# Sparse attention's pairs: the order of TensorE's step, and one PSUM bank for both heads of a narrow pair

## The chip, the cores and the metric

The kernel runs on one core of one Trainium2 chip. The metric is the time of an execution on the device in microseconds, the median of three. TensorE (PE), with its weight loads (PEld), VectorE (DVE), ScalarE (ACT), GpSimd (POOL) and SyncE (SP), which only issues transfers, run side by side and meet at semaphores.

## The reference

The program is two transformer blocks with several mixers, on 512 tokens of width 1024. The change touches one mixer of the second block, a sparse attention of 16 heads in 4 groups. It has three branches: over compressed blocks, over selected blocks, and over a window. With 512 tokens there are 8 blocks to select from and up to 16 are taken, and the window is 512 wide, so the selected and the window branch both come to causal attention over all keys, each with keys, values and a gate of its own. Cut to these two:

```python
q = q.reshape(B, S, G, Hg, dk) * dk ** -0.5            # 4 groups of 4 heads, dk = 64
gates = jax.nn.sigmoid(gl).reshape(B, S, G, Hg, 3)
...
p_sel = masked_softmax(jnp.einsum('bghtd,bgtkd->bghtk', qg, k_g), (pos <= t[:, None])[:, :, None])
o_sel = jnp.einsum('bghtk,bgtkd->btghd', p_sel.astype(v_g.dtype), v_g)
...
# the window: the same with k_w and v_w; then
# o = gates[0] * o_cmp + gates[1] * o_sel + gates[2] * o_win
```

## The kernel before

Everything is computed in fp32 with operands split into a high part (rounded) and a low part (the remainder), so that a product is made of two or three products of TensorE. In the stage in question (about 1034 to 1179 us of the profiled run) the work is cut into 64 **pairs**: the list `npairs` runs over 4 groups g, 4 query tiles t of 128 rows, 2 pairs of heads hp and the 2 branches b. Pair p has two heads, units 2p and 2p + 1 (`v_` in the code). A query tile t sees t + 1 key blocks of 128, so pairs 0 to 3 of a group work on 128 columns, 4 to 7 on 256, 8 to 11 on 384 and 12 to 15 on 512. The first two kinds are called narrow below, the others wide.

What happens to a pair, and the name of the semaphore that tells of it:

- `scores(p)` (PE): for each head two products for the high and low part of the keys and one that adds the mask, into one of two sets of PSUM banks, 0 and 1 or 2 and 3 (`p_scored`);
- reduce (DVE): the negative maximum over both heads (`p_peaked`);
- exponentials (ACT): one instruction for each head, which also sums (`p_exped`);
- scaling (POOL): the reciprocal of the sums, then one multiplication for each head (`p_scaled`);
- `turn(p)` (PE): transposes the t + 1 blocks of each head, the first head into bank 4, the second into bank 5, whatever the pair (`p_turned`);
- high (ACT): copies the transposed head, rounded, to `nprobT` (`p_high`); low (DVE): bank minus `nprobT` to `nprobL` (`p_low`), head by head; both tiles hold two pairs;
- `values(p)` (PE): products of both with the values, into banks 6 and 7, summed over the two branches (`p_summed`);
- after every second pair two additions (DVE) onto `oT`, which already holds the compressed branch (`p_added`).

There is no planner here: each engine has a loop written by hand over steps s, and its instructions run in that order. TensorE's step is values(s-4), scores(s+1), turn(s-2). ScalarE's is high(s-3), then the exponentials of s. VectorE's is reduce(s), low(s-3), and in even steps the additions. GpSimd goes through the heads one by one. `turn(p)` waits for the scaling of its head and for low of the same head of pair p-1, whose bank it writes. high(p) and low(p) also wait until values(p-2) have been computed, whose slot of `nprobT` and `nprobL` they overwrite. The stage before is the compressed branch, the one after it the output projection, whose weights are on their way already.

Of the kernel before, what the change touches and what calls it, by code (L numbers as in the profile page):

```python
# [23 lines left out]
ALU = mybir.AluOpType  # L24
ACT = mybir.ActivationFunctionType
AXX = mybir.AxisListType.X

P = 128
# [139 lines left out]
def build(nc, w, out):  # L168

    ctx = ExitStack()  # L170
    with ctx:
# [19 lines left out]
        bank = [psum[:, i, :] for i in range(8)]  # L191
# [16 lines left out]
        ident = const[:, C_ID:C_ID + P]  # L208
# [173 lines left out]
        class NormTiles:  # L382
# [60 lines left out]
            def turn(self, pe, t):  # L443

                for c in range(2):
                    pe.wait_ge(self.scaled, 2 * t + c + 1)
                    if t >= 2:
                        pe.wait_ge(self.low, 2 * (t - 2) + c + 1)
                    for i in range(4):
                        d = 4 * c + i  # L450
                        mm = nc.tensor.transpose(self.banks[2 * (t % 2) + c][:, i * P:(i + 1) * P],  # L451
                                                 self.h[:, t % 2, d * P:(d + 1) * P], ident)
                    mm.then_inc(self.turned, 1)
# [404 lines left out]
        for t in range(NT):  # L858
            for hp in range(FOX_H // 2):
                wd = (t + 1) * P  # L860
# [1469 lines left out]
        nprobL = nsa_tile("nprobL", [P, 4, S], 71424, F32R)  # L2330
        nprob = nsa_tile("nprob", [P, 8, S], 79616)
        nprobT = nsa_tile("nprobT", [P, 4, S], 96000, F32R)
# [406 lines left out]
        npairs = [(g, t, hp, b) for g in range(NSA_G) for t in range(NT) for hp in range(2) for b in range(2)]  # L2739
        n_np = len(npairs)  # L2740
# [11 lines left out]

        minus_one = stat[:, 36:38]

        def sum_of(o):
            return bank[6 + o % 2][:, 0:2 * P]

# [3 lines left out]
        @block.tensor  # L2761
        def _(pe):
            def scores(p):
                g, t, hp, b = npairs[p]
                wd = (t + 1) * P
                if p % 16 == 0:
                    pe.wait_ge(k_twice[g], 64)
                if p >= 2:
                    pe.wait_ge(p_exped, 2 * p - 2)
                for i in range(2):  # L2770
                    _, _, h, kb = unit_of(2 * p + i)
                    to = bank[2 * (p % 2) + i]
                    nc.tensor.matmul(to[:, 0:wd], lhsT=nq[:, h, q_tile(t)], rhs=hT[:, kb, 0:wd], start=True, stop=False)
                    nc.tensor.matmul(to[:, 0:wd], lhsT=nq[:, h, q_tile(t)], rhs=hL[:, kb, 0:wd], start=False, stop=False)
                    mm = nc.tensor.matmul(to[:, t * P:wd], lhsT=ident_r, rhs=mask_r, start=False, stop=True)
                mm.then_inc(p_scored, 1)

            def turn(p):
                t = npairs[p][1]
                for v_ in (2 * p, 2 * p + 1):  # L2780
                    pe.wait_ge(p_scaled, v_ + 1)
                    if v_ >= 2:
                        pe.wait_ge(p_low, v_ - 1)
                    for j in range(t + 1):
                        mm = nc.tensor.transpose(bank[4 + v_ % 2][:, j * P:(j + 1) * P], nprob[:, v_ % 8, j * P:(j + 1) * P], ident)  # L2785
                    mm.then_inc(p_turned, 1)

            def values(p):
                g, t, hp, b = npairs[p]
                o, kb = p // 2, 4 * b + g  # L2790
                if b == 0 and o >= 2:
                    pe.wait_ge(p_added, o - 1)
                pe.wait_ge(p_low, 2 * p + 2)
                to = sum_of(o).rearrange("p (h c) -> p h c", c=P)
                at_ = 2 * (p % 2)
                for j in range(t + 1):
                    cut = slice(j * P, (j + 1) * P)
                    first, last = b == 0 and j == 0, b == 1 and j == t
                    if not last:
                        mm = nc.tensor.matmul(to, lhsT=nv[:, j, kb, :], rhs=nprobT[:, at_:at_ + 2, cut], start=first, stop=False)  # L2800
                    mm = nc.tensor.matmul(to[0:HD], lhsT=nv[:, j, kb, 0:HD], rhs=nprobL[:, at_:at_ + 2, cut],
                                          start=False, stop=False)
                    if last:
                        mm = nc.tensor.matmul(to, lhsT=nv[:, j, kb, :], rhs=nprobT[:, at_:at_ + 2, cut], start=False, stop=True)
                mm.then_inc(p_summed, 1)

            scores(0)

            pe.wait_ge(c_done, 8)
            for s in range(n_np + 4):  # L2810
                if s >= 4:
                    values(s - 4)
                if s + 1 < n_np:
                    scores(s + 1)
                if 2 <= s < n_np + 2:
                    turn(s - 2)

        def chunk_high(a, c):
            a.wait_ge(p_added, 8 * (c // 2) + 8)
# [6 lines left out]
        @block.scalar  # L2826
        def _(a):
            for s in range(n_np + 3):
                for v_ in ((2 * s - 6, 2 * s - 5) if s >= 3 else ()):
                    t = npairs[v_ // 2][1]  # L2830
                    a.wait_ge(p_turned, v_ + 1)
                    if v_ >= 4:
                        a.wait_ge(p_summed, v_ // 2 - 1)
                    nc.scalar.activation(nprobT[:, v_ % 4, 0:(t + 1) * P], bank[4 + v_ % 2][:, 0:(t + 1) * P],
                                         ACT.Copy).then_inc(p_high, 1)
                if s < n_np:
                    wd = (npairs[s][1] + 1) * P
                    a.wait_ge(p_peaked, s + 1)
                    if s == 2:

                        a.wait_ge(k_low_g, NSA_G)
                    for i in range(2):
                        v_ = 2 * s + i
                        if v_ >= 8:
                            a.wait_ge(p_turned, v_ - 7)
                        if i == 0 and s >= 3:
                            a.wait_ge(p_inverted, s - 2)
                        nc.scalar.activation(nprob[:, v_ % 8, 0:wd], bank[2 * (s % 2) + i][:, 0:wd], ACT.Exp,
                                             bias=np_peak[s % 2][:, i:i + 1], accum_out=np_total[s % 3][:, i:i + 1]).then_inc(p_exped, 1)
                    for c in chunks_at(s):  # L2850
                        chunk_high(a, c)
            for c in (6, 7):
                chunk_high(a, c)

        @block.vector
        def _(v):
            link = Chain(v, p_chain)
            for s in range(n_np + 6):
                if s < n_np:
                    wd = (npairs[s][1] + 1) * P  # L2860
                    v.wait_ge(p_scored, s + 1)
                    if s >= 2:
                        v.wait_ge(p_exped, 2 * s - 2)
                    nc.vector.tensor_reduce(np_peak[s % 2], psum[:, 2 * (s % 2):2 * (s % 2) + 2, 0:wd], AXX,  # L2864
                                            ALU.max, negate=True).then_inc(p_peaked, 1)
                for v_ in ((2 * s - 6, 2 * s - 5) if 3 <= s < n_np + 3 else ()):
                    t = npairs[v_ // 2][1]
                    v.wait_ge(p_high, v_ + 1)
                    if v_ >= 4:
                        v.wait_ge(p_summed, v_ // 2 - 1)  # L2870
                    nc.vector.tensor_tensor(nprobL[:, v_ % 4, 0:(t + 1) * P], bank[4 + v_ % 2][:, 0:(t + 1) * P],  # L2871
                                            nprobT[:, v_ % 4, 0:(t + 1) * P], ALU.subtract).then_inc(p_low, 1)
                if s >= 6 and s % 2 == 0:

                    o = (s - 6) // 2
                    g, t, hp, _ = npairs[2 * o]
                    v.wait_ge(p_summed, 2 * o + 2)
                    if o == 0:
                        v.wait_ge(c_done, 8)
                    dst = oT[HD * hp:HD * hp + HD, 2 * g:2 * g + 2, q_tile(t)]  # L2880
                    src = sum_of(o).rearrange("p (h c) -> p h c", c=P)
                    link(nc.vector.tensor_tensor(dst, src[0:HD], dst, ALU.add))  # L2882
                    nc.vector.tensor_tensor(dst, src[HD:P], dst, ALU.add).then_inc(p_added, 1)
            for c in (6, 7):
                v.wait_ge(o_high, c + 1)
                nc.vector.tensor_tensor(hL[:, place[c], :], oT[:, c, :], hT[:, place[c], :], ALU.subtract).then_inc(o_low_v, 1)
# [336 lines left out]
```

## Time and profile before

| | us |
|---|---|
| median of 3 runs | 1748.11 (1747.83 to 1748.29) |
| the profiled execution | 1748.23, of which 1746.4 are the span of its instructions |
| granted clock of TensorE, mean | 0.995 of full |
| first scores of the stage to its last values | 1032.5 to 1179.1 |
| busy in the span: PE, PEld, DVE, ACT, POOL | 1712.6, 1522.1, 970.9, 825.4, 966.7 |

The rows further down are from views of one profiled execution. In a timeline a row is one instruction or several alike in a row (x2 and so on), with its start and its length; matmuls overlap in the pipeline, so the time that one takes up is read from start to start, not from its length. The clock is a share: 1.00 is 2.4 GHz and 0.50 is 1.2 GHz.

### The profile page before, as it was taken

What the parts mean: (1) busy time and instruction counts of PE and PEld (TensorE: products, weight loads), DVE (VectorE), ACT (ScalarE), POOL (GpSimd) and SP (SyncE); (2) the same over time, 40 slices, a digit from 0 to 9 for tenths busy, and PEclk for the clock granted to TensorE, in tenths of its full rate; (3) what the DMA queues carried; (4) which work ended last, traced back from release to release, by engine and by line L of the source; (5) the groups of instructions that cost most, each with busy time, mean ns of one, the idle gap of its engine ahead of it and who ended that gap; (6) DMA issues with size and microseconds to landing.
All of it is one profiled execution on the core that took longest, in us unless ns stands there. A gap on an engine that the chain in (4) does not pass through costs nothing.

```text
span 1746.4 us, 27720 instructions
## 1 busy us (share of the span) xinstructions
PE 1712.6 (98%) x10482; PEld 1522.1 (87%) x10482; DVE 970.9 (56%) x1638; ACT 825.4 (47%) x1667; POOL 966.7 (55%) x703
## 2 busy tenths in 40 slices
PE   8999999999999999999999999999999999999998
PEld 6988887888888998999888978888988889989996
DVE  4345664244438871586058469984333498428832
ACT  4224553232335552455256358874533556426642
POOL 4544332235444874677446459982842468638862
PEclk9999999999999999999999999999999999999999
DMA  6422122123351433233435330012531223323331
GB/s 226 119 76 60 49 73 58 49 61 98 113 169 49 121 115 115 73 97 116 127 91 148 97 107 3 6 33 73 169 109 61 77 69 107 124 73 109 110 121 48
DMA packets 222902, 161.57 MB, mean 93 GB/s; under 512 B 9769, under 2 KB 197425, under 8 KB 222770
## 3 DMA queue, kind: packets, MB, share of 16 engines
q1 hardware_dynamic: 221712, 158.73, 30.4%
q8 instruction: 84, 1.38, 0.3%
q10 hardware_dynamic: 1058, 1.07, 0.2%
q14 instruction: 48, 0.39, 0.1%
HBM read 155.57 MB, written 2.11 MB: 90 GB/s over the span
## 4 chain that ended last, share of the span: by engine, by line
PE 86%; DVE 8%; issue 3%; ACT 2%; POOL 1%; DMA 0%; DVEq 0%; SPq 0%; ACTq 0%
PE psum L365 26%; PE psum L367 26%; PE psum L366 26%; DVE nprobL L2871 2%; DVE stat L2864 1%; PE psum L1172 1%; PE psum L451 1%; PE psum L2785 1%; DVE ffn_quarters L2071 1%; PE psum L1183 1%; DVE ffn_tl L2081 1%; PE psum L1195 1%; PE psum L1249 1%; PE psum L1231 0%; DVE oT L2882 0%
## 5 line engine op out<-in xcount | busy, mean ns | idle before, releaser
L352 POOL TENSOR_TENSOR w_low<-ring,w_high 128x1024 fp32r<-128x1024 f32 (+2 forms) x223 | 488.7, 2202 | 537.5 <-ACT w_high L344 537.1
L365 PE MATMUL psum<-hT,w_high 128*128 128x256 f32 (+1 forms) x1120 | 380.8, 340 | 0.0
L367 PE MATMUL psum<-hT,w_low 128*128 128x256 f32 (+1 forms) x1120 | 375.2, 335 | 0.0
L366 PE MATMUL psum<-hL,w_high 128*128 128x256 f32 (+1 forms) x1120 | 375.2, 335 | 0.0
L344 ACT ACTIVATE w_high<-ring 128x1024 fp32r<-128x1024 f32 (+2 forms) x223 | 211.3, 953 | 298.6 <-PE psum L367 288.4
L367 PEld LDWEIGHTS psum<-hT,w_low 128*128 128x128 f32 x1120 | 212.6, 190 | 22.0
L365 PEld LDWEIGHTS psum<-hT,w_high 128*128 128x128 f32 x1120 | 212.9, 190 | 19.5 <-DVE hL L470 0.2
L366 PEld LDWEIGHTS psum<-hL,w_high 128*128 128x128 f32 x1120 | 212.9, 190 | 19.1
L1840 POOL TENSOR_TENSOR w_low<-ffn_sums,w_high 128x512 fp32r<-128x512 f32 x120 | 164.1, 1381 | 75.0 <-ACT w_high L1835 74.9
L1840 POOL TENSOR_TENSOR w_low<-ring,w_high 128x512 fp32r<-128x512 f32 x120 | 164.6, 1383 | 47.5 <-ACT w_high L1835 46.0
L365 PE MATMUL psum<-ffn_th,w_high 128*128 128x256 f32 x640 | 182.4, 285 | 5.5 <-POOL w_low L1840 2.8
L366 PE MATMUL psum<-ffn_tl,w_high 128*128 128x256 f32 x640 | 181.8, 284 | 0.0
L367 PE MATMUL psum<-ffn_th,w_low 128*128 128x256 f32 x640 | 181.8, 284 | 0.0
L759 DVE TENSOR_TENSOR x<-x,psum 128x512 f32<-128x512 f32 x56 | 36.0, 683 | 232.4 <-PE psum L367 232.4
L365 PE MATMUL psum<-w_high,ffn_act 128*128 128x512 f32 x352 | 137.2, 390 | 0.0
L366 PE MATMUL psum<-w_low,ffn_act 128*128 128x512 f32 x352 | 137.0, 389 | 0.0
L367 PE MATMUL psum<-w_high,ffn_act 128*128 128x512 f32 x352 | 137.0, 389 | 0.0
L365 PEld LDWEIGHTS psum<-ffn_th,w_high 128*128 128x128 f32 x640 | 123.5, 193 | 6.5 <-POOL w_low L1840 3.2
L366 PEld LDWEIGHTS psum<-ffn_tl,w_high 128*128 128x128 f32 x640 | 123.6, 193 | 0.0
L367 PEld LDWEIGHTS psum<-ffn_th,w_low 128*128 128x128 f32 x640 | 123.5, 193 | 0.0
L365 PE MATMUL psum<-w_high,hT 128*128 128x256 f32 (+2 forms) x320 | 105.8, 330 | 1.6 <-POOL w_low L352 0.9
L367 PE MATMUL psum<-w_high,hL 128*128 128x256 f32 (+2 forms) x320 | 104.8, 327 | 0.0
(447 smaller groups left out, 3723.4 us busy)
## 6 DMA issues: line engine op xcount, KB each, us to landing
ring<-in_w_in SPq DMA_DIRECT2D x58, 512.0 KB, 3.6
ring<-in_ffn_w_up SPq DMA_DIRECT2D x44, 512.0 KB, 3.8
ring<-in_w_gate SPq DMA_DIRECT2D x22, 512.0 KB, 3.8
ring<-in_w_up SPq DMA_DIRECT2D x22, 512.0 KB, 4.8
ring<-in_w_down SPq DMA_DIRECT2D x20, 512.0 KB, 4.0
ring<-in_ffn_w_down SPq DMA_DIRECT2D x20, 512.0 KB, 3.8
ring<-in_nsa_w_in SPq DMA_DIRECT2D x18, 512.0 KB, 3.6
ring<-in_ca_wkv SPq DMA_DIRECT2D x16, 512.0 KB, 3.7
```

Of the source, the lines that this page charges most:

```text
L344: nc.scalar.activation(tile_view(w_high, n, SPLIT), tile_view(ring, n, RING), ACT.Copy).then_inc(w_hi, 1)
L352: nc.gpsimd.tensor_tensor(tile_view(w_low, n, SPLIT), tile_view(ring, n, RING), tile_view(w_high, n, SPLIT), ALU.subtract).then_inc(w_lo, 1)
L365: nc.tensor.matmul(ps, lhsT=sh, rhs=mh, start=first, stop=False)
L366: nc.tensor.matmul(ps, lhsT=sh, rhs=ml_, start=False, stop=False)
L367: return nc.tensor.matmul(ps, lhsT=sl, rhs=mh, start=False, stop=last)
L451: mm = nc.tensor.transpose(self.banks[2 * (t % 2) + c][:, i * P:(i + 1) * P], self.h[:, t % 2, d * P:(d + 1) * P], ident)
L759: return nc.vector.tensor_tensor(dst, dst, ps, ALU.add)
L1172: mm = nc.tensor.matmul(bank[S0 + b][:, c0:c0 + cn], lhsT=lhsT, rhs=rhs, start=(j == 0), stop=(j == len(sc_) - 1))
L1183: mm = nc.tensor.transpose(bank[T0 + b][:, j * P:(j + 1) * P], pairs[p]["prob"][:, v_ % 4, c0:c0 + P], ident)
L1195: nc.tensor.matmul(to, lhsT=pairs[p]["probT"][:, v_ % 4, cut], rhs=val, start=(j == 0), stop=False)
L1840: nc.gpsimd.tensor_tensor(operand_place(w_low, r, j), self.source(r, name), operand_place(w_high, r, j), ALU.subtract).then_inc(u_low, 1)
L2871: nc.vector.tensor_tensor(nprobL[:, v_ % 4, 0:(t + 1) * P], bank[4 + v_ % 2][:, 0:(t + 1) * P], nprobT[:, v_ % 4, 0:(t + 1) * P], ALU.subt ...
```

## The change

Two things. TensorE's step becomes turn(s-2), values(s-4), scores(s+1). And the transposes of a narrow pair go into one bank, both heads side by side, bank 4 for even and bank 5 for odd pairs; ScalarE's and VectorE's copies of it are one instruction in place of two, and `turn(p)` then waits for low of pair p-2. Wide pairs keep a bank for each head and wait for low of the same head of pair p-1. Where narrow follows wide or wide follows narrow, both heads' low of the pair ahead is waited for.

```diff
--- before.py
+++ after.py
@@ -2752,6 +2752,22 @@
 
         minus_one = stat[:, 36:38]
 
+        def in_one(p):
+
+            return npairs[p][1] <= 1
+
+        def turned_to(v_):
+            p, wd = v_ // 2, (npairs[v_ // 2][1] + 1) * P
+            return bank[4 + p % 2][:, v_ % 2 * wd:v_ % 2 * wd + wd] if in_one(p) else bank[4 + v_ % 2][:, 0:wd]
+
+        def turned_heads(p):
+
+            wd = (npairs[p][1] + 1) * P
+            at_ = 2 * (p % 2)
+            if in_one(p):
+                return [(2 * p + 1, bank[4 + p % 2][:, 0:2 * wd].rearrange("p (h c) -> p h c", c=wd), slice(at_, at_ + 2), wd)]
+            return [(v_, turned_to(v_), v_ % 4, wd) for v_ in (2 * p, 2 * p + 1)]
+
         def sum_of(o):
             return bank[6 + o % 2][:, 0:2 * P]
 
@@ -2779,11 +2795,19 @@
                 t = npairs[p][1]
                 for v_ in (2 * p, 2 * p + 1):
                     pe.wait_ge(p_scaled, v_ + 1)
-                    if v_ >= 2:
+                    if p >= 1 and in_one(p) != in_one(p - 1):
+                        pe.wait_ge(p_low, 2 * p)
+                    elif p >= 2 and in_one(p):
+                        pe.wait_ge(p_low, 2 * p - 2)
+                    elif p >= 1:
                         pe.wait_ge(p_low, v_ - 1)
+                    to = turned_to(v_)
                     for j in range(t + 1):
-                        mm = nc.tensor.transpose(bank[4 + v_ % 2][:, j * P:(j + 1) * P], nprob[:, v_ % 8, j * P:(j + 1) * P], ident)
-                    mm.then_inc(p_turned, 1)
+                        mm = nc.tensor.transpose(to[:, j * P:(j + 1) * P], nprob[:, v_ % 8, j * P:(j + 1) * P], ident)
+                    if not in_one(p):
+                        mm.then_inc(p_turned, 1)
+                if in_one(p):
+                    mm.then_inc(p_turned, 2)
 
             def values(p):
                 g, t, hp, b = npairs[p]
@@ -2808,12 +2832,12 @@
 
             pe.wait_ge(c_done, 8)
             for s in range(n_np + 4):
+                if 2 <= s < n_np + 2:
+                    turn(s - 2)
                 if s >= 4:
                     values(s - 4)
                 if s + 1 < n_np:
                     scores(s + 1)
-                if 2 <= s < n_np + 2:
-                    turn(s - 2)
 
         def chunk_high(a, c):
             a.wait_ge(p_added, 8 * (c // 2) + 8)
@@ -2826,13 +2850,11 @@
         @block.scalar
         def _(a):
             for s in range(n_np + 3):
-                for v_ in ((2 * s - 6, 2 * s - 5) if s >= 3 else ()):
-                    t = npairs[v_ // 2][1]
+                for v_, src, at_, wd in turned_heads(s - 3) if s >= 3 else ():
                     a.wait_ge(p_turned, v_ + 1)
-                    if v_ >= 4:
-                        a.wait_ge(p_summed, v_ // 2 - 1)
-                    nc.scalar.activation(nprobT[:, v_ % 4, 0:(t + 1) * P], bank[4 + v_ % 2][:, 0:(t + 1) * P],
-                                         ACT.Copy).then_inc(p_high, 1)
+                    if s >= 5:
+                        a.wait_ge(p_summed, s - 4)
+                    nc.scalar.activation(nprobT[:, at_, 0:wd], src, ACT.Copy).then_inc(p_high, 2 if in_one(s - 3) else 1)
                 if s < n_np:
                     wd = (npairs[s][1] + 1) * P
                     a.wait_ge(p_peaked, s + 1)
@@ -2863,13 +2885,12 @@
                         v.wait_ge(p_exped, 2 * s - 2)
                     nc.vector.tensor_reduce(np_peak[s % 2], psum[:, 2 * (s % 2):2 * (s % 2) + 2, 0:wd], AXX,
                                             ALU.max, negate=True).then_inc(p_peaked, 1)
-                for v_ in ((2 * s - 6, 2 * s - 5) if 3 <= s < n_np + 3 else ()):
-                    t = npairs[v_ // 2][1]
+                for v_, src, at_, wd in turned_heads(s - 3) if 3 <= s < n_np + 3 else ():
                     v.wait_ge(p_high, v_ + 1)
-                    if v_ >= 4:
-                        v.wait_ge(p_summed, v_ // 2 - 1)
-                    nc.vector.tensor_tensor(nprobL[:, v_ % 4, 0:(t + 1) * P], bank[4 + v_ % 2][:, 0:(t + 1) * P],
-                                            nprobT[:, v_ % 4, 0:(t + 1) * P], ALU.subtract).then_inc(p_low, 1)
+                    if s >= 5:
+                        v.wait_ge(p_summed, s - 4)
+                    nc.vector.tensor_tensor(nprobL[:, at_, 0:wd], src, nprobT[:, at_, 0:wd],
+                                            ALU.subtract).then_inc(p_low, 2 if in_one(s - 3) else 1)
                 if s >= 6 and s % 2 == 0:
 
                     o = (s - 6) // 2
```

On TensorE, in step 11, of the first group: values of pair 7 (L2800, L2801, L2804), scores of pair 12 (L2773 to L2775) and the transposes of pair 9 (L2785, six blocks). Before:

```order
L2800 MATMUL psum<-nprobT,nv 128x256
L2801 MATMUL psum<-nprobL,nv 64x256 x2
L2804 MATMUL psum<-nprobT,nv 128x256
L2773 MATMUL psum<-hT,nq 128x512
L2774 MATMUL psum<-hL,nq 128x512
L2775 MATMUL psum<-const_r 128x128
L2773 MATMUL psum<-hT,nq 128x512
L2774 MATMUL psum<-hL,nq 128x512
L2775 MATMUL psum<-const_r 128x128
L2785 MATMUL psum<-const,nprob 128x128 x6
```

And now, with the transposes at L2806, values at L2824 to L2828, scores at L2789 to L2791:

```order
L2806 MATMUL psum<-const,nprob 128x128 x6
L2824 MATMUL psum<-nprobT,nv 128x256
L2825 MATMUL psum<-nprobL,nv 64x256 x2
L2828 MATMUL psum<-nprobT,nv 128x256
L2789 MATMUL psum<-hT,nq 128x512
L2790 MATMUL psum<-hL,nq 128x512
L2791 MATMUL psum<-const_r 128x128
L2789 MATMUL psum<-hT,nq 128x512
L2790 MATMUL psum<-hL,nq 128x512
L2791 MATMUL psum<-const_r 128x128
```

The transposes moved from behind the scores to ahead of the values; nothing else moved. On VectorE, at the passage from narrow to wide pairs in the first group, the rows of before are these: reduce is L2864, low is L2871 (of pairs 6, 7, 8 and 9, in steps 9 to 12), the additions are L2882 and L2883.

```order
L2864 TENSOR_REDUCE stat<-psum 128x2
L2871 TENSOR_TENSOR nprobL<-psum,nprobT 128x256 x2
L2864 TENSOR_REDUCE stat<-psum 128x2
L2871 TENSOR_TENSOR nprobL<-psum,nprobT 128x256 x2
L2882 TENSOR_TENSOR oT<-psum,oT 64x2x128
L2883 TENSOR_TENSOR oT<-psum,oT 64x2x128
L2864 TENSOR_REDUCE stat<-psum 128x2
L2871 TENSOR_TENSOR nprobL<-psum,nprobT 128x384 x2
L2864 TENSOR_REDUCE stat<-psum 128x2
L2871 TENSOR_TENSOR nprobL<-psum,nprobT 128x384 x2
```

In the changed kernel the same place reads: reduce is L2886, low is L2892, the additions are L2903 and L2904.

```order
L2886 TENSOR_REDUCE stat<-psum 128x2
L2892 TENSOR_TENSOR nprobL<-psum,nprobT 128x2x256
L2886 TENSOR_REDUCE stat<-psum 128x2
L2892 TENSOR_TENSOR nprobL<-psum,nprobT 128x2x256
L2903 TENSOR_TENSOR oT<-psum,oT 64x2x128
L2904 TENSOR_TENSOR oT<-psum,oT 64x2x128
L2886 TENSOR_REDUCE stat<-psum 128x2
L2892 TENSOR_TENSOR nprobL<-psum,nprobT 128x384 x2
L2886 TENSOR_REDUCE stat<-psum 128x2
L2892 TENSOR_TENSOR nprobL<-psum,nprobT 128x384 x2
```

The order on VectorE is that of before, reduce(s) ahead of low(s-3); only the two rows of low of a narrow pair have become one.

## Rows read from the trace of the kernel before

**Rows 1.** Busy time by stage, one period; columns: stretch, length, engines, clock, DMA.

```profile
1101.00:1136.00 35.00, 33.84 (x257) 30.95 (x258) 32.47 (x65) 29.94 (x100) 32.60 (x51) 1.00 0.04 15
```

**Rows 2.** Waits of the stage, 1034 to 1180 us: total, times, longest.

```profile
POOL stat L2898 <- ACT nprob L2848: 3.1, 6, 0.8
PE psum L2785 <- DVE nprobL L2871: 2.2, 6, 0.8
```

**Rows 3.** Timeline of TensorE, second group: start, length, operation, idle before.

```profile
1086.87 0.36 PE L2800 MATMUL psum<-nprobT,nv 128*128 128x256 f32 x1
...
1087.42 0.34 PE L2773 MATMUL psum<-hT,nq 128*128 128x384 f32 x1
...
1088.29 0.85 PE L2785 MATMUL psum<-const,nprob 128*128 128x128 f32 x6
...
1091.22 0.36 PE L2800 MATMUL psum<-nprobT,nv 128*128 128x256 f32 x1
...
1092.01 0.40 PE L2773 MATMUL psum<-hT,nq 128*128 128x512 f32 x1
...
1093.12 0.82 PE L2785 MATMUL psum<-const,nprob 128*128 128x128 f32 x6
...
1100.97 1.23 PE L2785 MATMUL psum<-const,nprob 128*128 128x128 f32 x8 [0.18 <-DVE nprobL L2871]
1101.95 0.36 PE L2800 MATMUL psum<-nprobT,nv 128*128 128x256 f32 x1
...
1102.97 0.22 PE L2773 MATMUL psum<-hT,nq 128*128 128x128 f32 x1
...
1103.58 1.06 PE L2785 MATMUL psum<-const,nprob 128*128 128x128 f32 x8
...
1110.42 0.22 PE L2775 MATMUL psum<-const_r 128*128 128x128 f32 x1
```

**Rows 4.** Timeline of VectorE, second group and end of the last.

```profile
1087.35 0.76 DVE L2871 TENSOR_TENSOR nprobL<-psum,nprobT 128x256 fp32r<-128x256 f32 x2
...
1088.92 0.96 DVE L2864 TENSOR_REDUCE stat<-psum 128x2 f32<-128x768 f32 x1
1089.79 1.01 DVE L2871 TENSOR_TENSOR nprobL<-psum,nprobT 128x384 fp32r<-128x384 f32 x2
...
1096.04 1.22 DVE L2864 TENSOR_REDUCE stat<-psum 128x2 f32<-128x1024 f32 x1
...
1100.14 1.28 DVE L2871 TENSOR_TENSOR nprobL<-psum,nprobT 128x512 fp32r<-128x512 f32 x2
...
1109.43 0.42 DVE L2864 TENSOR_REDUCE stat<-psum 128x2 f32<-128x256 f32 x1
1109.77 0.48 DVE L2871 TENSOR_TENSOR nprobL<-psum,nprobT 128x128 fp32r<-128x128 f32 x2
1110.68 0.69 DVE L2864 TENSOR_REDUCE stat<-psum 128x2 f32<-128x512 f32 x1 [0.44 <-PE psum L2775]
...
1157.30 0.76 DVE L2871 TENSOR_TENSOR nprobL<-psum,nprobT 128x256 fp32r<-128x256 f32 x2
...
1170.09 1.28 DVE L2871 TENSOR_TENSOR nprobL<-psum,nprobT 128x512 fp32r<-128x512 f32 x2
```

**Rows 5.** Busy time by stage: stretches elsewhere with TensorE idle.

```profile
272.00:275.00 3.00, 1.10 (x6) 0.68 (x6) 1.24 (x2) 1.64 (x3) 0.48 (x2) 0.98 0.00 0
275.00:278.00 3.00, 3.00 (x10) 2.32 (x10) 0.00 (x0) 0.39 (x1) 2.35 (x1) 0.50 0.00 0
279.00:282.00 3.00, 3.00 (x16) 2.35 (x15) 1.51 (x3) 0.68 (x3) 0.00 (x0) 1.00 0.51 151
1422.00:1425.00 3.00, 1.33 (x11) 1.12 (x10) 2.93 (x7) 2.23 (x5) 2.77 (x3) 1.00 0.28 76
```

**Rows 6.** Timeline of TensorE, start of the stage, clock at 0.50.

```profile
1040.65 0.56 PE L2800 MATMUL psum<-nprobT,nv 128*128 128x256 f32 x1
...
1041.22 0.42 PE L2773 MATMUL psum<-hT,nq 128*128 128x256 f32 x1
```

## The prediction

> **What bounds the kernel now.** I read the page's busy shares first: no engine stands out in the stretch that the diff touches, so I went to the busy time by stage. In one period of 16 pairs (35 us) TensorE is busy 33.8, GpSimd 32.6, VectorE 32.5 and ScalarE 29.9 us, with the clock at 1.00 [rows 1]. Four engines are nearly full at once. Such a stage is fast only while they overlap, and it can lose a great deal if two of them come to alternate. What can still be won is small: over all 64 pairs GpSimd, which works without a buffer to spare, waits 3.1 us for exponentials, and the transposes wait 2.2 us for VectorE [rows 2].
>
> The timeline of VectorE gives the period: low(7) of one group (pair numbers modulo 16 from here on) ends at 1087.35 + 0.76 = 1088.11, that of the group two further on at 1157.30 + 0.76 = 1158.06, so 34.98 us per group. From low(7) to the end of low(0) of the next group (1109.77 + 0.48 = 1110.25) it takes 22.14 us [rows 4]. These nine pairs, the eight wide ones and the first narrow one after them, are where the change acts.
>
> **The loop that closes.** Follow step s of the new order, for wide pairs. TensorE starts with turn(s-2), which must wait for low(s-3), head by head, since the wide pairs still have one bank for each head. Behind it in TensorE's queue stand values(s-4) and scores(s+1). VectorE's next step starts with the maximum of those scores, reduce(s+1), and only behind it stands low(s-2), for which turn(s-1) waits. So low, turn, values, scores, reduce, low is a closed chain with one pair per turn: TensorE rests while VectorE works and the other way round. Before, scores(s+1) stood ahead of turn(s-2); the chain went through the scores of the step after and covered two pairs.
>
> Narrow pairs escape it, because there turn(p) waits for low(p-2) only. Pairs 8 to 15 do not, nor does pair 0 of the next group: where the kind of bank changes, low of both heads of the pair ahead is waited for.
>
> **The price of one turn of the loop.** Pieces, all from start to start on the engine:
> - low's end to values' start, by way of the second head's turn: low of pair 12 ends at 1100.14 + 1.28 = 1101.42, values start at 1101.95: 0.53 us for four blocks [rows 3, 4]. About 0.10 of it is the way between engines (first head: 1100.14 + 0.69, turn at 1100.97), 0.43 the blocks. Three blocks: 0.43 in all. For pair 8 both heads wait: 0.76. For pair 0 one block for each head: 0.32.
> - values: 1 key block more each 0.23 or so: 0.55 (two blocks, 1086.87 to 1087.42), 0.79 (three, 1091.22 to 1092.01), 1.02 (four, 1101.95 to 1102.97) [rows 3].
> - scores: 0.87 (384 columns, 1087.42 to 1088.29), 1.11 (512, 1092.01 to 1093.12), 0.61 (128, 1102.97 to 1103.58) [rows 3].
> - scores' end to reduce: the mask product starts at 1110.42 and takes 0.22, reduce starts at 1110.68; 0.20 past the point to which I count scores [rows 3, 4].
> - reduce to low: 0.87 (1088.92 to 1089.79; its row says 0.96, so 0.09 overlaps), 1.22 - 0.09 = 1.13 for 1024 columns, 0.34 for 256 (1109.43 to 1109.77) [rows 4].
> - low of both heads: 1.01 (384), 1.28 (512) [rows 4]; for the narrow pair one instruction in place of two, which took 0.48 (1109.77); I keep 0.48 as its upper bound.
>
> The turn with pair q has values(q-2), scores(q+3), reduce(q+3):
> - q = 8: 0.76 + 0.55 + 0.87 + 0.20 + 0.87 + 1.01 = 4.26
> - q = 9: 0.43 + 0.55 + 1.11 + 0.20 + 1.13 + 1.01 = 4.43
> - q = 10 and 11: 0.43 + 0.79 + 1.11 + 0.20 + 1.13 + 1.01 = 4.67 each
> - q = 12: 0.53 + 0.79 + 1.11 + 0.20 + 1.13 + 1.28 = 5.04
> - q = 13: 0.53 + 0.79 + 0.61 + 0.20 + 0.34 + 1.28 = 3.75
> - q = 14 and 15: 0.53 + 1.02 + 0.61 + 0.20 + 0.34 + 1.28 = 3.98 each
> - q = 0 of the next group: 0.32 + 1.02 + 0.61 + 0.20 + 0.34 + 0.48 = 2.97
>
> Sum 37.75 in place of 22.14: +15.61, three times: **+46.8 us**. The last group has scores only up to q = 12: 23.07 in place of 13.31 (low(7) ends at 1158.06, low(12) at 1170.09 + 1.28 = 1171.37 [rows 4]): **+9.8**. Its last three turns have neither scores nor reduce; there values(q-2) now stands ahead of ScalarE's high(q), which needs the buffer that it frees: 0.79 + 1.02 + 1.02 = **+2.8**. ScalarE's copies and exponentials, GpSimd's scaling and the additions of VectorE lie within turns of 4 to 5 us, being 2 to 2.6 us of work per pair; if that cover went, they would show only above 4 us.
>
> The seven other pairs of a group, and the first eight, lose an instruction of ScalarE and one of VectorE per pair, a part of the 0.48 us [rows 4]. What that gives is bounded by zero below and by GpSimd's 3.1 us of waiting above [rows 2]; I take zero, since GpSimd keeps its pace whatever VectorE saves. The waits on transposes of both heads at once, for narrow pairs, cost a quarter of a microsecond of latency each and lie under GpSimd's queue; nothing. No DMA of the stage moves.
>
> At the full clock that makes 46.8 + 9.8 + 2.8 = +59.4: 1748.23, the profiled run's own time (the median is 1748.11), becomes 1807.6.
>
> **The clock.** TensorE would be at work for somewhat under half of each wide turn. What its clock does then, no row of before shows for certain. Where it was busy 1.10 of 3 us, it stood at 0.50 afterwards, the lower level (1.2 GHz); where it was busy 1.33 of 3 us, it stayed at 1.00 [rows 5]. At the lower level two products of 256 columns took 0.57 (1040.65 to 1041.22) where four take 0.55 [rows 3, 6]: the work doubles. TensorE's own part of the nine turns (transposes, values, scores) is 2.08 + 1.99 + 2.23 + 2.23 + 2.33 + 1.83 + 2.06 + 2.06 + 1.85 = 18.7 us, of the last five 10.9. If the clock stayed low through all of them: 3 x 18.7 + 10.9 = +67. If it never fell: 0. At half speed TensorE is busy for longer, so a fall tends to undo itself, as it did by 279 us [rows 5]; I take a quarter, **+17**, a choice between the bounds. Sum: 1748.2 + 59.4 + 17 = 1825, and I put 1822, giving the narrow pairs' saving a little.
>
> The Trainium skill ("TensorE: Matmul & The Clock Gate", section "A second HAM failure mode: psum-queue depth-cycling") says that a kernel whose TensorE pauses briefly between groups of matmuls as it goes round PSUM banks can see its clock swing between the two levels, and lose time to that. By this rule the sum is the one with the quarter, 1825; by the row that stayed at 1.00 [rows 5] it is 1807.6. The trace of before has the fall and the recovery but not the swing, as TensorE hardly pauses there.
>
> **The rivals.**
> - *The loop with the clock at full.* For: the row that stayed at 1.00 was fed no better. Against: the one that fell. 1807.6, with 4 us of error either way for the pieces, about 3% of the turns. Chance 0.22.
> - *The loop with the clock low for most of it.* Half to all of the 67: 1841 to 1874. Chance 0.13.
> - *Faster.* The turn comes first, so ScalarE and VectorE get their operand a values-and-scores earlier, and GpSimd's 3.1 us and the transposes' 2.2 us of waiting vanish [rows 2]: 1748.2 - 3.1 - 2.2 = 1743. It decides at one point: low(q-1) would have to end before TensorE is through with scores(q+2). But reduce(q+2) cannot start before those scores end, and low(q-1) is queued behind it; so for wide pairs it can't hold as the code stands, and is left only if I misread an order. Chance 0.03.
> - *It does nothing.* GpSimd's 32.6 of 35 us [rows 1] set the pace as before and the new waits stay below its queue: 1748. For: GpSimd's pace is the tightest of the narrow pairs. Against: a wide pair would have to get through the chain in the present 22.14 / 9 = 2.46 us, and reduce and low alone take 2.41 of it at 512 columns. Chance 0.03.
>
> **How the numbers follow.** The likeliest is the loop with the clock falling now and then, between 1812 and 1840: chance 0.59, 1822. With the loop at full clock it holds 0.81; the range 1798 to 1848 covers both and the first part of the low-clock case. Measurements of this kernel tell some 0.2% (3.5 us) from nothing. Slower holds three of the cases, 0.94; same 0.03; faster 0.03.
>
> **What would show it.** Right: in the wide stretches of the new profile the transposes wait for VectorE's low, and reduce for the mask product, each about 2 us a pair, where before these waits are tenths; the nine pairs take some 37 to 45 us in place of 22; GpSimd's wait for exponentials grows to tens of us; narrow pairs keep their pace. The granted clock of the wide stretches settles the second term. Wrong: if low for a wide pair ends before the scores of the same step, if the wide pairs keep 2.5 us each, or if the loss stands in the narrow pairs.

## The result, and the profile after

The changed kernel takes 1841.54 us (median of 4 runs, 1840.19 to 1845.36) against 1748.20 in the same session (1747.83 to 1749.78): a ratio of 1.0536 [1.0524, 1.0548]. It is slower, by 93 us; the forecast was 1822, in a range from 1798 to 1848. The profiled execution took 1845.36 (span 1843.6), the one of before 1748.23: 97.1 us to account for.

First the waits of the changed kernel in the stage, 1030 to 1280 us (total, times, longest); they answer to [rows 2]. L2886 is now reduce, L2892 low, L2806 the transposes, L2791 the mask product, L2857 high, L2870 the exponentials, L2919 and L2921 GpSimd's scaling.

```profile
DVE stat L2886 <- PE psum L2791: 100.8, 47, 4.2
POOL stat L2919 <- ACT nprob L2870: 91.3, 38, 4.8
...
PE psum L2806 <- DVE nprobL L2892: 56.7, 33, 2.2
ACT nprob L2870 <- DVE stat L2886: 54.5, 49, 2.4
```

VectorE and TensorE wait for each other: reduce for the mask product 47 times, 2.1 us each on average; the transposes for low 33 times, 1.7 us each. GpSimd waits 91.3 us where it waited 3.1. I take that for a consequence: it has nothing to scale until these two have gone round.

Next the busy time of the changed kernel by stretch, answering to [rows 1]: the wide pairs of the four groups, then the narrow pairs behind the second (stretch, length, busy TensorE, weight loads, VectorE, ScalarE, GpSimd; clock; the last two columns are of the transfers).

```profile
1057.00:1103.00 46.00, 32.08 (x180) 28.80 (x181) 20.59 (x37) 18.67 (x55) 18.66 (x29) 0.81 0.00 0
1118.00:1164.00 46.00, 32.31 (x177) 29.07 (x178) 20.28 (x36) 18.95 (x55) 19.41 (x29) 0.74 0.00 1
1179.00:1221.00 42.00, 28.09 (x179) 25.04 (x180) 20.58 (x37) 19.38 (x57) 19.69 (x30) 0.88 0.11 38
1236.00:1275.00 39.00, 25.41 (x142) 21.69 (x142) 17.78 (x30) 15.95 (x40) 14.79 (x20) 0.82 0.00 1
1164.00:1179.00 15.00, 11.57 (x81) 9.64 (x79) 11.66 (x21) 10.69 (x37) 13.09 (x21) 1.00 0.01 2
```

VectorE, ScalarE and GpSimd are each busy less than half of a wide stretch. TensorE looks busier than it is at work, since its granted clock is 0.74 to 0.88 there and the same work takes longer; in the narrow pairs it is at 1.00.

Now VectorE's timeline in the second group of the changed kernel (start, length, operation, idle before): the loop at full clock, at half clock, and the last narrow pair of the group.

```profile
1117.09 0.68 DVE L2892 TENSOR_TENSOR nprobL<-psum,nprobT 128x512 fp32r<-128x512 f32 x1
...
1120.15 0.96 DVE L2886 TENSOR_REDUCE stat<-psum 128x2 f32<-128x768 f32 x1 [1.59 <-PE psum L2791]
1121.02 1.01 DVE L2892 TENSOR_TENSOR nprobL<-psum,nprobT 128x384 fp32r<-128x384 f32 x2
1124.30 1.23 DVE L2886 TENSOR_REDUCE stat<-psum 128x2 f32<-128x1024 f32 x1 [2.27 <-PE psum L2791]
1125.44 1.01 DVE L2892 TENSOR_TENSOR nprobL<-psum,nprobT 128x384 fp32r<-128x384 f32 x2
...
1141.89 1.23 DVE L2886 TENSOR_REDUCE stat<-psum 128x2 f32<-128x1024 f32 x1 [4.18 <-PE psum L2791]
1143.03 1.28 DVE L2892 TENSOR_TENSOR nprobL<-psum,nprobT 128x512 fp32r<-128x512 f32 x2
1148.29 0.42 DVE L2886 TENSOR_REDUCE stat<-psum 128x2 f32<-128x256 f32 x1 [3.98 <-PE psum L2791]
1148.63 1.28 DVE L2892 TENSOR_TENSOR nprobL<-psum,nprobT 128x512 fp32r<-128x512 f32 x2
...
1177.52 0.96 DVE L2886 TENSOR_REDUCE stat<-psum 128x2 f32<-128x768 f32 x1 [1.04 <-PE psum L2791]
1178.39 0.68 DVE L2892 TENSOR_TENSOR nprobL<-psum,nprobT 128x512 fp32r<-128x512 f32 x1
```

And TensorE's, of the changed kernel, for the same turns:

```profile
1121.71 0.99 PE L2806 MATMUL psum<-const,nprob 128*128 128x128 f32 x6 [1.60 <-DVE nprobL L2892]
1122.45 0.36 PE L2824 MATMUL psum<-nprobT,nv 128*128 128x256 f32 x1
...
1124.04 0.22 PE L2791 MATMUL psum<-const_r 128*128 128x128 f32 x1
1126.13 0.98 PE L2806 MATMUL psum<-const,nprob 128*128 128x128 f32 x6 [1.87 <-DVE nprobL L2892]
...
1143.86 1.94 PE L2806 MATMUL psum<-const,nprob 128*128 128x128 f32 x8 [2.01 <-DVE nprobL L2892]
1145.45 0.56 PE L2824 MATMUL psum<-nprobT,nv 128*128 128x256 f32 x1
...
1175.16 0.97 PE L2806 MATMUL psum<-const,nprob 128*128 128x128 f32 x4 [0.79 <-POOL nprob L2921]
```

Low's end, transposes, values, scores, reduce, low: each end of a wait is the start of the other engine's work, where [rows 3, 4] had tenths. Low of pair 7 ends at 1117.09 + 0.68 = 1117.77, of pair 8 at 1122.03, of pair 9 at 1126.45: turns of 4.26 and 4.42. At 1143.86 eight blocks take 1.59 to the start of values, where they took 0.98 before [rows 3]: from 1140 to 1149 us the granted clock is 0.50, where it was 1.00 from 1117 to 1131.

From the ends of low on VectorE the whole difference can be told (us; the fourth column is the execution of the fifth experiment below, in which the clock stays at full):

| stretch | before | after | filled | forecast at full clock |
|---|---|---|---|---|
| start to low(7) of the first group | 1053.14 | 1057.08 | 1054.27 | 1053.14 |
| low(7) to low(0), three groups | 22.13, 22.14, 22.13 | 45.51, 46.07, 41.65 | 39.61, 38.05, 38.03 | 37.75 each |
| low(0) to low(7), three times | 12.84 each | 15.18, 15.23, 15.18 | 15.16, 15.18, 15.16 | 12.84 each |
| last low(7) to the last low | 19.81 | 39.13 | 34.15 | 32.4 |

After less before: +3.9, +66.8, +7.1 and +19.3, together 97.1.

### The profile page after: what moved, and what is told of

Read it like the earlier page. It is cut to its first block, busy times and chain, and to the rows that moved or that the text cites. A ratio compares the mean times of both kernels' runs of the same rounds, so it can differ in the third digit from the quotient of the medians.

```text
span 1843.6 us, 27601 instructions
## 1 busy us (share of the span) xinstructions
PE 1745.6 (95%) x10482; PEld 1547.1 (84%) x10482; DVE 970.4 (53%) x1606; ACT 824.5 (45%) x1635; POOL 967.6 (52%) x703
## 4 chain that ended last, share of the span: by engine, by line
PE 87%; DVE 6%; issue 3%; POOL 2%; ACT 2%; DMA 0%; DVEq 0%; SPq 0%; ACTq 0%; POOLq 0%
PE psum L365 25%; PE psum L366 24%; PE psum L367 24%; PE psum L2806 2%; DVE nprobL L2892 1%; POOL nprob L2921 1%; PE psum L1172 1%; PE psum L2825 1%; PE psum L2789 1%; PE psum L2790 1%; PE psum L2824 1%; PE psum L451 1%; DVE ffn_quarters L2071 1%; POOL stat L2919 1%; PE psum L1183 1%
## 5 line engine op out<-in xcount | busy, mean ns | idle before, releaser
L2806 PE MATMUL psum<-const,nprob 128*128 128x128 f32 x320 | 62.7, 321 | 70.1 <-DVE nprobL L2892 56.7
L2806 PEld LDWEIGHTS psum<-const,nprob 128*128 128x128 f32 x320 | 40.0, 159 | 86.8 <-issue 66.5
```

The source lines that it names most:

```text
L2806: mm = nc.tensor.transpose(to[:, j * P:(j + 1) * P], nprob[:, v_ % 8, j * P:(j + 1) * P], ident)
```

## The experiments

**The order alone, the bank alone, by kind of pair.** Four kernels. The first is the kernel before with the new order and two banks for every pair.

```diff
             for s in range(n_np + 4):
+                if 2 <= s < n_np + 2:
+                    turn(s - 2)
                 if s >= 4:
                     values(s - 4)
                 if s + 1 < n_np:
                     scores(s + 1)
-                if 2 <= s < n_np + 2:
-                    turn(s - 2)
```

> Only the new order of TensorE's step; every head keeps its own bank and its own copies, as before. The loop theory (low, turn, values, scores, reduce, low with one pair per turn) says that now the narrow pairs run in it too: some 2.2 us a pair at 128 columns and 3.2 at 256, against 1.6 to 1.9 before, so about 7 us a group where the changed kernel lost 2.4; the wide pairs as in the changed kernel: 1850 to 1868 us. The theory that the one bank for both heads is to blame says 1748.

Measured: 1888.18 (1878.01 to 1898.34, 2 runs), ratio 1.0804 [1.0749, 1.0858]: above the expectation. The narrow stretches took 22.9, 29.1 and 29.2 us, in place of 12.84: 10 to 16 us more a group, where I had priced about 7. Busy time of this kernel in them, columns as above:

```profile
1110.00:1132.00 22.00, 13.35 (x87) 11.80 (x86) 11.48 (x26) 11.09 (x42) 14.00 (x22) 0.92 0.00 1
1179.00:1208.00 29.00, 19.88 (x89) 18.35 (x89) 12.03 (x28) 12.05 (x44) 14.03 (x22) 0.56 0.00 1
1258.00:1286.00 28.00, 19.60 (x88) 17.88 (x86) 11.23 (x25) 11.17 (x41) 14.04 (x22) 0.56 0.00 1
```

With two banks the loop holds the narrow pairs too: in the second of these stretches reduce waits 7 times for the mask product (16.8 us) and the transposes 8 times for low (9.9 us). In the second and third the clock falls to 0.56. The shared bank of the change does loosen the narrow pairs.

The second undoes the order and keeps the shared bank (the diff above, the other way round, on the changed kernel).

> Only one bank for both heads of a narrow pair, with the copies and waits that go with it; TensorE's step in the old order. The loop theory: no loop over one pair is closed, so 1745 to 1748.5 us, the saving bounded by GpSimd's 3.1 us of waiting. The one-bank theory: most of the loss stays, 1810 to 1841.

Measured: 1751.02 (1747.39 to 1754.00, 11 runs), 1.0017 [1.0008, 1.0026], 2.8 us slower than before, and 2.5 above the expected upper end. Low(0) to low(7) takes 13.56, 0.72 more than before, the wide stretch 22.04. One instruction of 256 columns in place of two of 128 won nothing that the end sees.

The third turns only narrow pairs first, the fourth only wide pairs.

```diff
-                if 2 <= s < n_np + 2:
+                early = 2 <= s < n_np + 2 and in_one(s - 2)
+                if early:
                     turn(s - 2)
...
+                if 2 <= s < n_np + 2 and not early:
+                    turn(s - 2)
```

> The changed kernel, but only narrow pairs are turned first in TensorE's step; wide pairs are turned last, as before. The loop theory: the wide pairs take 22 us again for nine, and only what the narrow pairs and the start lost in the changed kernel stays (7.1 + 3.9 us): 1752 to 1762. If the loss were in the narrow pairs' new waits and dragged the wide ones along: above 1800.

Measured: 1763.57 (1759.51 to 1764.33), 1.0086 [1.0072, 1.0100], just above the expected upper end. Low(0) to low(7) takes 15.18, as in the changed kernel; the nine pairs take 23.45, 1.3 more than before.

The fourth has `not in_one(s - 2)` in that place.

> The counterpart of the run that turned only narrow pairs first: the changed kernel, but only wide pairs are turned first, narrow ones last, as before. If the losses are separate and add up, this lacks only what the turned order costs the narrow pairs and the start (1.6 us in each of three groups and 1.6 at the start): 1828 to 1841 us, the clock's swings included. If the narrow pairs' order fed the wide loop's loss, the wide pairs get shorter too: below 1820.

Measured: 1831.99 (1825.78 to 1834.51), 1.0475 [1.0447, 1.0504]. The parts add up to within 3 us: 15.3 for narrow pairs first, 83.8 for wide ones, less the 2.8 of the bank that stands in both, make 96.3; the changed kernel lost 93.3. Most of the loss comes from the wide pairs.

**Is it the loop through VectorE's queue?** If reduce ahead of low closes the loop, low ahead of reduce should open it.

```diff
             for s in range(n_np + 6):
+                for v_, src, at_, wd in turned_heads(s - 3) if 3 <= s < n_np + 3 else ():
...
+                                            ALU.subtract).then_inc(p_low, 2 if in_one(s - 3) else 1)
                 if s < n_np:
                     wd = (npairs[s][1] + 1) * P
...
-                for v_, src, at_, wd in turned_heads(s - 3) if 3 <= s < n_np + 3 else ():
```

> The changed kernel with two pieces of VectorE's step swapped: low(s-3) ahead of reduce(s). The loop theory: scores and reduce leave the loop; what remains is turn, values, high, low, some 3 us a wide pair in place of 4 to 5 and more, with the clock up again: 1765 to 1795. A theory that has ScalarE's high waiting for the values as the cause, or the one bank, says that this changes nothing or makes it worse: 1835 to 1855.

Measured: 1833.96 (1833.81 to 1834.12, 2 runs), 1.0493 [1.0474, 1.0513]. This is 39 us above the expected upper end, and 1 us from the range that the other theories named (1835 to 1855); the time alone speaks for them. VectorE's timeline of this kernel in the second group (here L2885 is low, L2892 reduce):

```profile
1131.51 1.02 DVE L2885 TENSOR_TENSOR nprobL<-psum,nprobT 128x384 fp32r<-128x384 f32 x2 [0.98 <-ACT nprobT L2857]
1132.45 1.22 DVE L2892 TENSOR_REDUCE stat<-psum 128x2 f32<-128x1024 f32 x1
1135.56 1.02 DVE L2885 TENSOR_TENSOR nprobL<-psum,nprobT 128x384 fp32r<-128x384 f32 x2 [1.89 <-ACT nprobT L2857]
```

and ScalarE's of the same kernel:

```profile
1133.70 0.69 ACT L2870 ACTIVATE nprob<-psum,stat 128x512 f32<-128x512 f32 x1 [1.84 <-DVE stat L2892]
...
1135.04 0.87 ACT L2857 ACTIVATE nprobT<-psum 128x384 fp32r<-128x384 f32 x2
```

Low, reduce, exponentials, high, low: 1131.51 to 1135.56, 4.05 us, again a closed chain of one pair, now between VectorE and ScalarE, since high(s-2) is queued behind exp(s), which waits for reduce(s), which waits behind low(s-3). I had looked at TensorE's waits only. The run says that this swap on VectorE does not mend the step; it does not test the first loop. Whether high waiting for the values is the cause instead is tested two experiments further on.

**What is in the loop, and what isn't.** If the loop is as told, then work of VectorE that lies between reduce and low costs its full length, and the same work behind low nothing, as VectorE is half idle. Twenty reductions (five for each group) whose results nobody reads, in one place or the other:

```diff
                                             ALU.max, negate=True).then_inc(p_peaked, 1)
+                if s < n_np and s % 16 >= 11:
+                    nc.vector.tensor_reduce(stat[:, 40 + 2 * (5 * (s // 16) + s % 16 - 11):42 + 2 * (5 * (s // 16) + s % 16 - 11)], nv[:, 0, :, :].rearrange("p (a b) c -> p a (b c)", a=2), AXX, ALU.max)
                 for v_, src, at_, wd in turned_heads(s - 3) if 3 <= s < n_np + 3 else ():
```

> The changed kernel with one more reduction of 1024 columns from SBUF (about 1.1 us) on VectorE in 20 steps, those of the wide loop, between reduce and low; its result is read by nobody. VectorE is idle for half of these steps. The loop theory: between reduce and low it is in the loop all the same, 20 x 1.1 us: 1858 to 1878. A theory of filled engines says that an engine half idle takes it for nothing: 1841.

Measured: 1880.16 (1878.82 to 1880.82), 1.0763 [1.0747, 1.0779], 38.6 more than the changed kernel and 2 above the expected upper end. One row groups the added instructions, another is the first wide stretch of this kernel:

```profile
L2889 DVE TENSOR_REDUCE stat<-nv x20: 1207/1210/1220, 1059.2 to 1293.4; 128x2 f32<-128x1024 f32 x20
1055.00:1111.00 56.00, 35.62 (x180) 32.49 (x181) 26.83 (x42) 19.65 (x58) 19.28 (x30) 0.73 0.00 0
```

20 x 1.21 = 24.2 is the work itself. The other 14.4 stand beside a lower clock (mean 0.966 against 0.977 over the profiled execution, 0.73 against 0.81 in the first wide stretch); that the clock is all of them is not shown.

The same reductions at the end of VectorE's step, behind low and the additions:

> The same 20 reductions, but at the end of VectorE's step, behind low and the additions, where VectorE waits for the next scores. The loop theory: nothing or nearly, 1839 to 1848. If VectorE's load counted, the same as with the reduction between reduce and low.

Measured: 1841.97 (1839.66 to 1848.16), 1.0541 [1.0523, 1.0558]; the changed kernel took 1841.54. The 24 us of work cost nothing there. So the way from reduce to low on VectorE lies in the chain that sets the time, and what follows low there does not.

**Values out of the loop.** Step turn, scores, values:

```diff
                     turn(s - 2)
-                if s >= 4:
-                    values(s - 4)
                 if s + 1 < n_np:
                     scores(s + 1)
+                if s >= 4:
+                    values(s - 4)
```

> The changed kernel with TensorE's step as turn, scores, values. The loop theory: values leave the loop over low, turn, scores, reduce, but ScalarE's high then comes still later, behind the values; by the same rows as in the prediction the nine pairs take 34.3 in place of 37.8 us at the full clock, 14 us less in all, and a little more from the clock: 1810 to 1832. The rival that high waiting for the values is the cause says slower: 1850 to 1875.

Measured: 1829.45 (1823.29 to 1831.12), 1.0467 [1.0447, 1.0488], 12 us better than the changed kernel and near the upper end of what was expected. Had high's wait for the values been the cause, it would have been slower (1850 to 1875). ScalarE's timeline of this kernel shows the wait that comes in place of the one removed:

```profile
1121.89 0.87 ACT L2857 ACTIVATE nprobT<-psum 128x384 fp32r<-128x384 f32 x2 [1.94 <-PE psum L2828]
```

The transposes of pair 9 start at 1119.19 and those of pair 10 at 1123.14, 3.95 apart, where the changed kernel has 4.42 (1121.71 to 1126.13): 0.47 of the 0.55 that values take. High now waits for values to free its buffer. The nine pairs took 40.6 to 42.5 us and not the 34.3 of the expectation, which was for the full clock: the granted clock of this kernel's wide stretches was 0.83 to 0.88 in the first three groups. In the last it was 1.00, and low(7) to the last low took 31.9 us where the filled kernel below needs 34.15.

**The clock by itself.** If the loop pauses TensorE and its clock falls for that, then work in the pauses should give it back. Ten products of 256 columns behind the scores, in the steps that turn a wide pair, into columns that nobody reads:

```diff
+            def fill(s):
+
+                o = (s - 4) // 2 + s % 2
+                for _ in range(10):
+                    nc.tensor.matmul(bank[6 + o % 2][:, 2 * P:4 * P], lhsT=ident_r, rhs=hT[:, 0, 0:2 * P], start=s % 2 == 1, stop=s % 2 == 1)
+
...
+                if 4 <= s < n_np and not in_one(s - 2):
+                    fill(s)
```

> The changed kernel plus work for nobody: in each step whose transposes are of a wide pair, TensorE runs ten more products of 256 columns behind the scores (about 1.2 us at the full clock), into columns of banks 6 and 7 that nobody reads. If TensorE waits there for VectorE by some 2 us a step and its clock falls because of these waits, the extra work lies in the wait, keeps the clock up, and the kernel gets faster: 1806 to 1825 us. If TensorE's own work sets the pace of the wide pairs, 30 steps or so pay 1.2 us each: 1865 to 1885. If the clock has nothing to do with it: 1836 to 1847.

Measured: 1821.65 (1819.91 to 1822.93), 1.0428 [1.0413, 1.0444], 20 us better than the changed kernel with more work. Its wide stretches, columns as above:

```profile
1055.00:1094.00 39.00, 35.20 (x257) 32.08 (x256) 19.81 (x35) 17.87 (x52) 17.75 (x28) 0.96 0.00 1
1109.00:1147.00 38.00, 34.01 (x256) 30.91 (x257) 20.45 (x37) 18.88 (x55) 19.60 (x30) 1.00 0.01 1
1162.00:1200.00 38.00, 33.79 (x254) 30.70 (x255) 20.47 (x37) 18.91 (x54) 19.83 (x30) 1.00 0.11 43
1215.00:1250.00 35.00, 28.18 (x204) 24.91 (x205) 18.73 (x32) 16.50 (x41) 15.28 (x21) 1.00 0.00 1
```

From the second group on the clock is at 1.00, and the loop runs at 38.05 and 38.03 for nine pairs. No kernel here beat the one before.

## Why the prediction was right, and where it was off

**The loop.** Right in place, order and size. Turns of the changed kernel at full clock took 4.26 (pair 8), 4.42 (9) and 4.78 (10), forecast as 4.26, 4.43 and 4.67; the two filled groups at 1.00 took 38.04 for the 37.75 of the sum. The sum used pieces of the kernel before alone, from start to start (one was misread: the way from low's end to the next transposes, "about 0.10", is 0.14 by its own rows, 1100.83 to 1100.97; the sum hardly moves). The waits came where it put them, and the two placements of the same reductions show that the chain, and not how full VectorE is, sets the time.

**The clock.** Forecast +17, between 0 and 67; the medians with and without filling differ by 20, the two profiled executions by 25.4, of which 22.5 stand in the wide stretches. Where the clock stands at 0.50, the doubling of TensorE's part explains the turns to hundredths: pair 12 took 7.39 (low ends at 1136.92 and 1144.31), forecast 5.04 + 2.33 = 7.37; pair 13 took 5.60, forecast 3.75 + 1.83 = 5.58. How often it falls I had chosen, a quarter of the bound, without a row that priced it; it is near a third (20 to 22.5 of 67), and that the choice came so near is partly luck. The rule from the Trainium skill that was weighed beside it ("TensorE: Matmul & The Clock Gate", section "A second HAM failure mode: psum-queue depth-cycling") agrees with the trace: pauses of 1.60 and 1.87 us as TensorE goes round the banks, and the clock of the wide stretches goes up and down, to means of 0.74 to 0.88.

**The step that failed: narrow pairs and the start at zero.** They cost 7.1 and 3.9 us, where the prediction put nothing and then took 3 us off its sum of 1825 for a saving there. The reason given, that GpSimd keeps its pace, held nearly: from the scaling of pair 3 to that of pair 8 it took 1175.60 - 1164.44 = 11.16 us, where it took 10.60. GpSimd's timeline in the changed kernel:

```profile
1164.44 0.70 POOL L2919 TENSOR_TENSOR stat<-stat 128x2 f32<-128x2 f32 x1 [3.60 <-ACT nprob L2870]
...
1175.60 0.70 POOL L2919 TENSOR_TENSOR stat<-stat 128x2 f32<-128x2 f32 x1
```

and in the kernel before, same pairs:

```profile
1110.78 0.70 POOL L2898 TENSOR_TENSOR stat<-stat 128x2 f32<-128x2 f32 x1 [0.53 <-ACT nprob L2848]
...
1121.38 0.70 POOL L2898 TENSOR_TENSOR stat<-stat 128x2 f32<-128x2 f32 x1
```

But the wide stretch starts from low(7), not from GpSimd. Before, low(7) ended 1.71 us after GpSimd began pair 8 (1123.09 - 1121.38), and now 3.47 (1179.07 - 1175.60). In the changed kernel turn(7) starts at 1175.16, behind it stand values(5) and scores(10), then reduce(10) at 1177.52, and only then low(7) at 1178.39: the loop's first turn begins one narrow pair earlier than I counted. That is 1.76 of the 2.39 per group, GpSimd's pace 0.56, the rest before pair 3. With the bank alone 0.72 of the 2.39 are there; with narrow pairs turned first all but 0.05 (15.18), so the rest comes with the order.

The start varies from run to run, from 1.1 us in the filled kernel to 5.1 in one with added reductions, but the variation stands ahead of the stage. The first reduce of the stage in the kernel before, the changed one and the filled one:

```profile
1034.07 0.41 DVE L2864 TENSOR_REDUCE stat<-psum 128x2 f32<-128x256 f32 x1
...
1034.39 0.41 DVE L2886 TENSOR_REDUCE stat<-psum 128x2 f32<-128x256 f32 x1
...
1031.60 0.41 DVE L2894 TENSOR_REDUCE stat<-psum 128x2 f32<-128x256 f32 x1
```

From there to the end of low(7), by the first line of the table, it takes 19.07 us before, 22.69 in the changed kernel and 22.67 in the filled one; 22.69 and 22.68 with the added reductions, 22.69 with only narrow pairs turned first, and 19.82 with the bank alone. So with narrow pairs turned first and one bank the first eight pairs cost 3.6 us in every one of these runs; 0.75 of it stands with the bank alone, the rest comes with the order. Why the stage itself begins up to 2.5 us earlier or 3.2 later than before is open.

The last group at full clock took 34.15, 1.7 over the forecast, and 1.6 of this stands in its last three turns: in the filled kernel low(12) ends at 1238.65 and low(15) at 1249.61, 10.96 us, where 6.50 + 2.83 were forecast. The forecast added values alone to each old turn. In the last turn before, high started 0.21 us after low of pair 14 ended (1175.74 to 1175.95); in the filled kernel the transposes of both heads (0.53) and the values (1.02) lie between, and it starts 1.81 after (1245.88 to 1247.69).

So at full clock the loss was 71.7 (1819.91 - 1748.23) where 59.4 were forecast: +2.5 from the wide pairs (1.6 of it in the first group, whose clock was 0.96), +1.7 from the last group, +7.0 and +3.6 from what was put at zero, less the 2.5 by which the stage of this execution began earlier.

**The rivals.** Faster, and nothing: excluded, for the reason given (low of a wide pair never ended before the scores of its step). The loop at full clock: it is what the filled kernel shows, 1821.65 and not 1807.6. The clock low for most of the stage: by its time alone the changed kernel could be this one, since 1841.54 lies 1.5 above the 1840 that bounded the likeliest case and at the 1841 where this rival begins. The clock decides: with means of 0.74 to 0.88, where 0.50 is the lower level, it was low for about a quarter to a half of the wide stretches, and it was the costs put at zero that brought the time there. The kernel with the order alone came near this rival in the narrow pairs (0.56).

## What to carry to other kernels

Before an instruction moves within an in-order step, go round each chain of waits, count the pairs that one round covers, in every engine's queue, and price the round piece by piece: here the move took the lead from two pairs to one, and the nine pairs from 2.46 to 4.2 us each at full clock while VectorE, ScalarE and GpSimd became about half idle. Also count the round that leads into the stretch and the one that leads out. Whether work lies in the loop can be tested directly: the same extra instruction costs at least its length there (38.6 us for 24.2 of work here) and nothing just behind it.

## What the runs showed of the hardware that I had not expected

More work on TensorE made the kernel faster: ten added products in each wide step took it from 1841.54 to 1821.65 us, as the granted clock of the wide stretches rose from between 0.74 and 0.88 to between 0.96 and 1.00. And in the kernel with the order alone the clock was at 0.56 over stretches where TensorE was busy 19.9 of 29 us: the prediction had supposed that a fall undoes itself, since TensorE is busy for longer at half clock, and there it did not.
